# Down projection: stores of the last sums two part loads sooner in SP's queue, and the lower halves of the first 16 parts in four pieces

## What is computed

```python
def swiglu(hn, w_gate, w_up, w_down):
    return (jax.nn.silu(hn @ w_gate) * (hn @ w_up)) @ w_down
...
        h = h + swiglu(rms_norm(h, norm_ffn_g[l]), w_gate[l], w_up[l], w_down[l])
    return rms_norm(h, norm_final_g)
```

## Time and profile before

| | us |
|---|---|
| median of 3 runs | 2901.45 (2899.13 to 2903.7) |
| the profiled execution | 2901.37 |
| its span | 2899.6 |
| PE busy | 2862.3 (99%) |
| DVE busy | 1851.6 (64%) |
| ACT busy | 1146.5 (40%) |
| POOL busy | 1468.4 (51%) |
| share of PE in the chain that ended last | 93% |

### The profile page before, as it was taken

How to read it: one execution, slowest core, us unless ns; L and a number is a source line. 1 busy time by engine, 2 the same in 40 slices (tenths; PEclk the granted TensorE clock), 3 DMA queues, 4 the chain that set the end, 5 groups by cost and what they waited for, 6 DMA issues and landing times.

```text
span 2899.6 us, 41618 instructions
## 1 busy us (share of the span) xinstructions
PE 2862.3 (99%) x14070; PEld 2405.0 (83%) x14070; DVE 1851.6 (64%) x2620; ACT 1146.5 (40%) x2049; POOL 1468.4 (51%) x1214
## 2 busy tenths in 40 slices
PE   8999999999999999999999999999999999999998
PEld 8888888888888888887888888888888888888786
DVE  2564566656359777777877456665634866665778
ACT  5522455424244333334543245543423433333334
POOL 7422455452235555568972244455222655456886
PEclk9999999999999999999999999999999999999999
DMA  7623222241113444467644332225112223324764
GB/s 255 214 94 105 92 87 76 69 177 44 59 73 135 161 146 156 166 230 246 228 136 145 108 97 79 76 74 177 52 45 79 81 105 109 109 93 143 258 195 167
DMA packets 179231, 372.68 MB, mean 129 GB/s; under 512 B 17105, under 2 KB 58129, under 8 KB 179089
## 3 DMA queue, kind: packets, MB, share of 16 engines
q1 hardware_dynamic: 116592, 301.06, 30.4%
q10 hardware_dynamic: 62496, 69.78, 7.1%
HBM read 268.51 MB, written 102.27 MB: 128 GB/s over the span
## 4 chain that ended last, share of the span: by engine, by line
PE 93%; DVE 3%; DMA 1%; POOL 1%; issue 1%; ACT 1%; SPq 0%; DVEq 0%; ACTq 0%; POOLq 0%
PE PS L3018 19%; PE PS L3020 18%; PE PS L3019 18%; PE PS L3389 9%; PE PS L1999 2%; PE PS L2003 2%; PE PS L2001 2%; PE PS L1972 2%; PE PS L1970 2%; PE PS L1971 2%; PE PS L3052 2%; PE PS L3056 2%; PE PS L3054 2%; PE PS L1909 1%; PE PS L1887 1%; PE PS L3034 1%
## 5 line engine op out<-in xcount | busy, mean ns | idle before, releaser
L782 POOL TENSOR_TENSOR down_lo<-down_raw,down_hi 128x1024 fp32r<-128x1024 f32 (+1 forms) x196 | 390.5, 2026 | 49.4 <-ACT down_hi L1262 49.1
L2360 POOL TENSOR_TENSOR w_lo<-raw,w_hi 128x256 fp32r<-128x256 f32 (+1 forms) x144 | 197.4, 1385 | 348.1 <-ACT w_hi L2453 348.1
L748 POOL TENSOR_TENSOR part_lo<-sum_s,part_hi 128x512 fp32r<-128x512 f32 x176 | 235.4, 1344 | 226.7 <-ACT part_hi L1242 226.2
L1719 DVE TENSOR_TENSOR copied<-copied,PS 128x512 f32<-128x512 f32 x264 | 177.6, 687 | 230.7 <-PE PS L3020 221.5
L3018 PE MATMUL PS<-op_t_hi,part_hi 128*128 128x512 f32 x704 | 274.7, 390 | 0.3 <-issue 0.2
L3020 PE MATMUL PS<-op_t_hi,part_lo 128*128 128x512 f32 x704 | 274.3, 390 | 0.0
L3019 PE MATMUL PS<-op_t_lo,part_hi 128*128 128x512 f32 x704 | 274.3, 390 | 0.0
L1803 DVE TENSOR_TENSOR h<-h,PS 128x512 f32<-128x512 f32 x344 | 218.5, 681 | 60.6 <-PE PS L3020 45.0
L3018 PE MATMUL PS<-act_hi,w_hi 128*128 128x512 f32 (+1 forms) x696 | 253.6, 364 | 0.7 <-POOL w_lo L2335 0.4
L1262 ACT ACTIVATE down_hi<-down_raw 128x1024 fp32r<-128x1024 f32 x154 | 159.1, 1057 | 240.1 <-PE PS L3020 141.2
L3019 PE MATMUL PS<-act_lo,w_hi 128*128 128x512 f32 (+1 forms) x696 | 251.8, 362 | 0.0
(11 more groups left out here) (372 smaller groups left out, 7083.9 us busy)
## 6 DMA issues: line engine op xcount, KB each, us to landing
raw<-in_w_units SPq DMA_DIRECT2D x132, 512.0 KB, 4.0
a_d<-copied SPq DMA_DIRECT2D x154, 256.0 KB, 2.2
down_raw<-a_d SPq DMA_DIRECT2D x154, 256.0 KB, 3.5
gu_raw<-in_w_units SPq DMA_DIRECT2D x44, 512.0 KB, 4.5
down_raw<-t_d SPq DMA_DIRECT2D x88, 256.0 KB, 3.0
down_raw<-in_w_units SPq DMA_DIRECT2D x66, 256.0 KB, 2.8
qkvz_d<-stage ACTq DMA_DIRECT2D x64, 256.0 KB, 2.4
raw<-att_d SPq DMA_DIRECT2D x32, 512.0 KB, 3.3
```

The costliest lines, as they stand in the source:

```text
L748: pool.tensor_tensor(lo[:, :], part_source(s, k), hi[:, :].bitcast(f32), ALU.subtract)\
L782: last = pool.tensor_tensor(flat(lo[:, :, :])[:, cs], flat(down_raw[m % 4][:, :, :])[:, cs], flat(hi[:, :, :])[:, cs].bitcast(f32), ALU.su ...
L1719: dve.tensor_tensor(buf[dst][:, :], buf[a][:, :], bank(k), ALU.add)\
L2360: last = pool.tensor_tensor(w_lo[slot][:, cs], raw[raw_slot][:, cs], w_hi[slot][:, cs].bitcast(f32), ALU.subtract)
```

## The change

There are two edits. `store_sums` of the last pair stands behind the load of part 13 instead of part 15. And `down_lo` makes the lower half of parts 0 to 15 in four instructions of 256 columns instead of one of 1024; parts 16 to 55 keep one, the later ones two. The semaphore is raised by the last piece, as before. Both hold in both halves.

```diff
 LO_PIECES = 2
+EARLY_PIECES = 4
...
             pool.wait_ge(S["w_hi_ready"], down_no(half, m) + 1)
-            pieces = LO_PIECES if m >= FIRST_TRIPLE else 1
+            pieces = LO_PIECES if m >= FIRST_TRIPLE else EARLY_PIECES if m < 16 else 1
             for i in range(pieces):
...
                 store_products(last, of_f(half, last, 1, 2, 2), 1)
-                load_parts(10, 16)
+                load_parts(10, 14)
                 store_sums(last, s_count(half, last, 4), 1)
+                load_parts(14, 16)
                 sp.wait_ge(S["a_stored0"], rows_stored(half, NPAIR, 0))
                 sp.wait_ge(S["a_stored1"], rows_stored(half, NPAIR, 1))
```

## The result

The changed kernel is slower: median 2910.57 us (2909.09 to 2910.97) against 2900.73 us (2899.13 to 2903.7) for the kernel before on the same chip, a ratio of 1.0033 with a 95% interval of 1.0024 to 1.0042 (ratios here are of the means, so they can differ a little from those of the medians). The forecast of 2896.8 and the range up to 2901.8 both miss, and on the other side. The profiled execution took 2910.44 us (span 2908.7, 9.1 more than before).

The account below looks back on a forecast made before the run. TensorE, busy 99% of the span, was taken as the bound, with 8.9 us of waits to recover. Gains of 4.40 us (first half) and 0.16 (second), 4.6 in all, off 2901.37 gave 2896.8 us; range 2892.0 to 2901.8.

Parts of the forecast that it names:

- The two places of the purse: PE's waits in the last pair's down projection: 6.35 us lost in the first half, 2.56 in the second, 8.9 in all.
- the row sums as the second half's cause: Second half: two DVE row sums of 2.84 and 2.86 us make PE stand still, 2.56 us together.
- POOL's price: Lower halves on POOL: four 256-column pieces take 2.84 us a part back to back, where a whole part costs 2.40.
- Rival (3): POOL overrun at 3.24 us a part, reload later, PE loses 19.2 us against 8.9: 2911 us; chance 0.07.
- with 256-column pieces it should take at most about 0.69 + 0.7 = 1.4 us: A DVE row sum meeting POOL's pieces: at most about 1.4 us, against 2.84 beside a whole part.
- two products, three row sums: Five DVE row operations taken to get in between POOL's instructions in this stretch, each pushing POOL by 0.45 us.
- the other price: A DVE row sum meeting 512-column pieces in POOL was taken to last 1.78 us, the basis for the 1.4 us.
- I priced the fall at nothing: First half: PE's clock would hold behind the new wait, saving the 2.80 us lost at the lower clock.
- the predicted 1.95 us: First half: PE would run dry at 1319.45 and resume at 1321.4, losing 1.95 us where it lost 3.55.
- that costs 0 to 1.2 us, and I take 0.6: Delay of the reload of h rows 4 to 7 by part 15's load right ahead of it in the DMA engines.
- the 1312.8 worked out for the move alone: First half: moved stores by themselves would allow the reload's issue at about 1312.8, where it was 1317.32.
- The forecast's own spread: Total time 2894.8 to 2898.5 us, from the 0 to 1.2 us of the queue in both halves.

Follow-up runs that it names:

- the stores alone: Moved stores only, lower halves of parts 0 to 15 left whole, against the kernel before: 2897.81 us against 2900.12, ratio 0.9988.
- the first run with pieces from part 4: The changed kernel with parts 0 to 3 whole and four pieces only from part 4, first of two runs of the same code: 2903.41 us.
- the three runs with the reload first: Moved stores, part 15's load behind the reload of h rows 4 to 7; two pieces 2895.9 us, whole parts 2896.36, four pieces from part 9 2896.19.
- pieces alone: Four pieces for parts 0 to 15, stores left where the kernel before has them: 2911.96 us, ratio 1.0040.

## Why the prediction was wrong

**What held.** The two places of the purse, the row sums as the second half's cause, and POOL's price: 25.02 us for nine parts (2.78 each) in the second half, 2.82 in the first, beside a predicted 2.84. Rival (3), an overrun POOL, gave nearly the right time, 2911, for a reason that was not there, which is luck. The run in which POOL waits for its own piece (about 3.15 us a part, 2911.05 us) shows what it would have looked like.

**The step that failed** is "with 256-column pieces it should take at most about 0.69 + 0.7 = 1.4 us". It was right for the row sums (0.68 to 1.06 us after), which met POOL in the first four pieces after a break, or standing still. It was carried over to the products, which come 14.0 us into an unbroken run. I had counted them among the operations that get in between ("two products, three row sums", at 0.45 us each) and never asked what if one does not. The copies of step 0 behind them on the DVE, on which PE hangs, stood in no term of the sum. The Trainium skill ("SBUF — State Buffer", section "SBUF: two separate sides") has the later of the two engines blocked until the first one's instruction is finished; by that the product would have got in at the next piece, 0.35 us on. The trace shows it blocked over 16 further instructions. The row behind the other price, 1.78 us beside 512-column pieces, is of an addition of the same shape and not of a row sum; the runs with two pieces bear it out (row sums of 0.67 to 1.76 us).

**The clock.** I priced the fall at nothing since it had held behind an idle 1.80 us elsewhere. In this place it doesn't hold so long: in the stores alone the idle was 1.58 us and the clock stayed at 1.00, in the first run with pieces from part 4 it was 1.81 us and the next 6.2 us ran at 0.72. Four other waits of 2.14, 2.57, 3.30 and 3.34 us had 0.72, 0.72, 0.72 and 0.74 behind them; two of 1.06 and 1.30 us held it at 1.00. So even with prompt products the predicted 1.95 us, between 1.81 and 2.14, would most likely have cost a fall. It is not certain: further on in the same stage, in the three runs with the reload first, PE stood idle for 1.95, 1.96 and 1.97 us, and the clock fell behind the 1.95 us alone.

```profile
1321.50:1327.70 6.20, 6.16 (x20) 4.90 (x21) 6.12 (x11) 0.00 (x0) 2.58 (x4) 0.72 1.01 374
```

That stretch has 20 matmuls where 27.4 fit: 1.7 us.

**The reload's queue.** The term "that costs 0 to 1.2 us, and I take 0.6" was mis-sized: 8.6 − 6.0 = 2.6 us in the first half, 9.4 against 6.5 = 2.9 in the second, with the loads of parts 14 and 15 in flight ahead. With the load of part 15 behind it the reload took 6.2 and 6.6 with two pieces and 6.6 and 7.3 with whole parts, but 8.9 and 8.4 with pieces from part 9, so that the order in the queue is not all of it. Two terms of the forecast thus had the wrong size beside the step that was missing, and in the run of the stores alone the second is plain: its reload goes out at 1313.08, close to the 1312.8 worked out for the move alone, and the DVE gets it 7.6 us later instead of 4.95.

**The spread.** The forecast's own spread, 2894.8 to 2898.5, doesn't follow from the 0 to 1.2 us that it names: with 0.6 already counted in each half, that gives 2895.6 to 2898.0. The chance of a time below 2895.6 was set a little too high by it.

**What is shown and what isn't.** Shown: the pieces cause the loss (with and without the moved stores); it comes with pieces of 256 and of 341 and 342 columns and not with 512; it does not hang on the DVE's operation or size, nor on the place within the piece; a break between POOL's pieces lets the DVE in. Not shown: the rule by which one attempt gets in and the next doesn't. In runs of narrow pieces only, every attempt up to the 11th piece got in and all from the 16th on failed; where whole parts came first the border was blurred (3rd and 7th narrow in, 4th and 7th out), and behind an entry even the 20th got in. What these cases suggest is that the distance to the DVE's last entry counts, 3 us in and 6 us out; no run varied that distance alone, and it doesn't decide between the 7th pieces.

## What to carry to other kernels

Cutting one engine's instructions smaller lets the other in more often only if the other gets the seams, and here it did not. Before pricing such a cut, look for every two-SBUF operation of the DVE that falls into the run, what is queued behind it, and how long the run is without a break; wide pieces, or cutting only the part of the run that the short operations meet (here from part 9), were safe in these runs. And a moved DMA issue has two ends: what the loads now ahead of it do to a large transfer can take back most of what the earlier issue gives.

## What the runs showed of the hardware

- A DVE instruction with two SBUF inputs, even over one column, can be kept out by back-to-back POOL instructions of 342 columns or fewer for the rest of the run: 9.5 to 12.3 us here, past a whole part of 1024 columns among them, until POOL stood still. In runs of 512 columns or more only it always got in at a seam.
- An entry costs POOL 0.45 us, as worked out: the piece that meets it takes 1.14 to 1.22 us instead of 0.74 (changed kernel and first run with pieces from part 4; less where the two overlap only in part). A one-column operation that got in cost POOL nothing.
- A semaphore wait of POOL on its own last piece costs 0.12 us a piece (0.815 between starts, 0.70 without).
- PE fell to the lower clock behind idles from 1.81 us on in the down projection, and it held behind 1.58 us there. Further on in the same stage it held behind 1.97 us (1.00 over the next 6.2 us, two pieces with the reload first) and fell behind 1.95 us (0.72, whole parts with the reload first). The length of the idle alone does not decide.
- The reload of two times 1 MB took 6.0 to 6.5 us to land with no other DMA of the queue in flight at its issue (kernel before, pieces alone), 6.2 to 8.9 us with part 14's two loads of 256 KB in flight, and 6.8 to 9.4 us where part 15's were in flight as well.
